# Two chained transformer blocks on one core: modulation sums moved ahead, first weights in places of their own

## The reference

```python
mod = c @ w_ada[l] + b_ada[l]                       # 1024 -> 6 * 1024, one vector
shift_m, scale_m, gate_m, shift_f, scale_f, gate_f = jnp.split(mod, 6, axis=-1)
h = modulate(rms_norm(x, g_pre_mix[l]), shift_m, scale_m)
proj = h @ w_in[l]                                  # q_a k_a v_a q_m k_m v_m o_m i_m f_m g_a g_m
...                                                 # rope, window attention; conv, silu, mLSTM
merged = sigmoid(g_a) * (y_a @ w_branch_attn[l]) + sigmoid(g_m) * (y_m @ w_branch_mlstm[l])
x = x + gate_m[:, None, :] * rms_norm(merged @ w_out[l], g_post_mix[l])
h2 = modulate(rms_norm(x, g_pre_ffn[l]), shift_f, scale_f)
ff = (silu(h2 @ w_ffn_gate[l]) * (h2 @ w_ffn_up[l])) @ w_ffn_down[l]
```

## Time and profile before

| | |
|---|---|
| median of 3 runs | 824.28 us (822.32 to 824.84) |
| the profiled execution | 825.46 us, of which the span of its trace is 823.7 us |
| PE busy | 773.9 us (94%) |
| DVE busy | 638.8 us (78%) |
| ACT busy | 393.4 us (48%) |
| moved from HBM | 171.60 MB, 210 GB/s over the span |

### The profile page before, as it was taken

How to read it: one execution, slowest core, us unless ns; L and a number is a source line. 1 busy time by engine, 2 the same in 40 slices (tenths; PEclk the granted TensorE clock), 3 DMA queues, 4 the chain that set the end, 5 groups by cost and what they waited for, 6 DMA issues and landing times.

```text
span 823.7 us, 15888 instructions
## 1 busy us (share of the span) xinstructions
PE 773.9 (94%) x6624; PEld 708.5 (86%) x6624; DVE 638.8 (78%) x840; ACT 393.4 (48%) x552; POOL 29.0 (4%) x44
## 2 busy tenths in 40 slices
PE   2879998999999999999999999989998999999996
PEld 2779988989878899999887988889878999999874
DVE  5857988988986987868886999886599777555456
ACT  3346755484455355443444795542225544444440
POOL 0200000000001000000001000040010000000000
PEclk9789999998999999999999999999999999999999
DMA  9794677583574999888992743600364679565621
GB/s 356 247 351 128 205 245 245 176 282 116 168 253 155 317 327 351 276 282 318 341 364 72 262 129 111 218 8 3 104 210 124 206 230 340 176 202 188 198 100 51
DMA packets 96021, 173.68 MB, mean 211 GB/s; under 512 B 7767, under 2 KB 55230, under 8 KB 95950
## 3 DMA queue, kind: packets, MB, share of 16 engines
q1 hardware_dynamic: 92848, 165.87, 60.7%
q0 software_dynamic: 1872, 5.86, 2.3%
q10 hardware_dynamic: 1230, 0.95, 0.3%
HBM read 171.60 MB, written 1.05 MB: 210 GB/s over the span
## 4 chain that ended last, share of the span: by engine, by line
PE 70%; DVE 18%; ACT 4%; DMA 3%; issue 3%; ACTq 1%; DVEq 0%; SPq 0%; POOL 0%; POOLq 0%
PE bank L2063 13%; PE bank L2064 12%; PE bank L2065 12%; PE bank L2328 4%; PE bank L2330 4%; PE bank L2329 4%; DVE wlo L448 3%; PE bank L2038 2%; PE bank L2039 2%; PE bank L2040 2%; DVE acc L475 2%; PE bank L2490 1%; DMA raw<-in_w_in 1%; DVE arena L475 1%; ACT whi L625 1%
## 5 line engine op out<-in xcount | busy, mean ns | idle before, releaser
L625 ACT ACTIVATE whi<-raw 128x1024 fp32r<-128x1024 f32 (+2 forms) x220 | 225.7, 1036 | 250.1 <-PE bank L2065 110.3
L448 DVE TENSOR_TENSOR wlo<-raw,whi 128x1024 fp32r<-128x1024 f32 (+2 forms) x220 | 259.7, 1195 | 94.3 <-ACT whi L625 90.6
L2063 PE MATMUL bank<-hh,whi 128*128 128x256 f32 x1016 | 287.0, 282 | 11.6 <-DVE wlo L448 8.6
L2064 PE MATMUL bank<-hl,whi 128*128 128x256 f32 x1016 | 284.2, 280 | 0.0
L2065 PE MATMUL bank<-hh,wlo 128*128 128x256 f32 x1016 | 284.1, 280 | 0.0
L2063 PEld LDWEIGHTS bank<-hh,whi 128*128 128x128 f32 x1016 | 192.8, 190 | 15.7 <-DVE wlo L448 7.8
L2064 PEld LDWEIGHTS bank<-hl,whi 128*128 128x128 f32 x1016 | 192.6, 190 | 0.5 <-issue 0.5
L2065 PEld LDWEIGHTS bank<-hh,wlo 128*128 128x128 f32 x1016 | 192.7, 190 | 0.0
L475 DVE SCALAR_TENSOR_TENSOR acc<-raw,cc,acc 128x1024 f32<-128x1024 f32 x56 | 71.7, 1281 | 6.1 <-DMA raw<-in_w_ada 3.7
L2328 PE MATMUL bank<-whi,ffh 128*128 128x512 f32 x168 | 65.7, 391 | 0.9 <-DVE wlo L448 0.9
L2330 PE MATMUL bank<-whi,ffl 128*128 128x512 f32 x168 | 65.5, 390 | 0.0
(11 more groups left out here) (445 smaller groups left out, 1051.7 us busy)
## 6 DMA issues: line engine op xcount, KB each, us to landing
raw<-in_w_ada SPq DMA_DIRECT2D x96, 512.0 KB, 5.2
raw<-in_w_in SPq DMA_DIRECT2D x54, 512.0 KB, 4.6
raw<-in_w_ffn_in SPq DMA_DIRECT2D x88, 256.0 KB, 3.9
raw<-in_w_ffn_gate SPq DMA_DIRECT2D x44, 256.0 KB, 4.5
raw<-in_w_ffn_up SPq DMA_DIRECT2D x44, 256.0 KB, 5.5
raw<-in_w_ffn_down SPq DMA_DIRECT2D x22, 512.0 KB, 5.3
raw<-in_w_ffn_out SPq DMA_DIRECT2D x22, 512.0 KB, 4.3
raw<-in_w_out SPq DMA_DIRECT2D x16, 512.0 KB, 4.4
```

The lines of the kernel that those rows point to most:

```text
L448: eng.tensor_tensor(lo[:, 0:nk * width], raw[:, b % RAW, 0:nk * width], hi[:, 0:nk * width].bitcast(fp), ALU.subtract)\
L625: act.activation(weight_place(g)[0][:, 0:nk * width], raw[:, b % RAW, 0:nk * width], ACT.Copy)\
L2063: mm(o, wh[:, k, c], xh[:, kk_, :], start=first, stop=False)
L2064: mm(o, wh[:, k, c], xl[:, kk_, :], start=False, stop=False)
```

## The change

It has five parts.

1. The 8 weight blocks of `o_if` get places of their own in a part of the arena that is free then (`FIRST = 8`), so their high halves wait for nothing, and the four shared places begin with `qm`.
2. `head` puts `c4` (part 2, first half) beside `qm`, `c5` beside `km`, `c6` and `c7` (part 3) beside `g2` and `g3`, `c8` beside `ba0`. Nothing stands beside `kva` and `g1`.
3. PE sums part 2 behind `g1` instead of behind `g2`, with 16 idle products around it, and part 3 behind `wo1` instead of ahead of `ba0`.
4. The constants and small vectors are issued by SP, two ahead of each of blocks 28 to 36, instead of by ACT; `x` is issued behind six blocks instead of two. ACT takes two small copies (`v1T`, `bmod`) from DVE.
5. The order ahead of `ba0` changes on PE, ACT and DVE, and there are fewer idle products at three places (`run_on` 22 to 16, 9 to 7, 18 to 13).

```diff
-    head = ["c0", "c1", "c2", "c3", "o_if", "qm", "km", "vm", "g0", "qa", "kva", "c8", "g1", "c4", "g2", "c5",
-            "g3", "c6", "ba0", "c7", "ba1", "bm0", "bm1", "wo0", "c9", "wo1"]
+    head = ["c0", "c1", "c2", "c3", "o_if", "qm", "c4", "km", "c5", "vm", "g0", "qa", "kva", "g1", "g2", "c6",
+            "g3", "c7", "ba0", "c8", "ba1", "bm0", "bm1", "wo0", "c9", "wo1"]
...
+        FIRST = 8
         def weight_place(g):
+            if g < FIRST:
+                at = [2112 + 576 * i for i in range(12)] + [15680 + 576 * i for i in range(4)]
+                return tuple(rounded(f"first{i}", at[i], [576]) for i in (2 * g, 2 * g + 1))
...
             for b, (_, _, nk, width, parts, _, _) in enumerate(order):
-                if b == 2:
+                if b == 6:
                     sp.dma_start(xt[:, :, :], A["x"][0].rearrange("(m p) n -> p m n", p=P)).then_inc(sem("x_in"), 16)
...
+                if 28 <= b < 37:
+                    for n in (2 * (b - 28), 2 * (b - 28) + 1):
+                        small_transfer(n)
...
-                    elif g >= HL:
+                    elif g >= HL + FIRST:
...
-            act.dma_start(cst[:, 258:CONST_N], A["const"][:, 258:CONST_N]).then_inc(sem("const_in"), 16)
-            act.dma_start(cc[:, 1, :], A["c_2"][0].rearrange("(p k) -> p k", k=8)).then_inc(sem("small_in"), 16)
-            vectors(1, ROWS2, v2)
...
-            scale_h(0, second_half)
-            prepare("o_if", slice(2, 4))
+            scale_h(0, second_half, lambda: prepare("o_if", slice(2, 4)))
...
+            part(2, lambda: run_on(4, 6))
+            run_on(4, 6)
             pe.wait_ge(sem("qr_ready"), 2)
...
-            pe.wait_ge(sem("piece_used"), 4)
-            intra_part(1, 4)
+            inter_part(1)
             turn_ya(1)
-            inter_part(1)
...
             rows_out("wo1", merged)
-            turn_h(1, lambda m: xn[:, m * D:(m + 1) * D], "xn_ready", 2, 18, 2 * (place["wo1"][0] % 2))
+            part(3)
+            turn_h(1, lambda m: xn[:, m * D:(m + 1) * D], "xn_ready", 2, 13, 2 * (place["wo1"][0] % 2))
```

More of the change, by code:

```diff
@@ L182, in build @@
         hreg = sb("hreg", [P, 4096])
+        made = {}
         def rounded(name, at, shape):
-            return nc.alloc_sbuf_tensor_at(name, [P] + shape, fr, offset=arena_at + 4 * at)
+            if name not in made:
+                made[name] = nc.alloc_sbuf_tensor_at(name, [P] + shape, fr, offset=arena_at + 4 * at)
+            return made[name]
         hh = rounded("hh", ARENA, [KT, S])
@@ L664, in _ @@
                    .then_inc(sem("xn_ready"), 1)
+            act.wait_ge(sem("vec_turned"), 2)
+            act.activation(v1T[:, :], bank[2][:, 0:n1], ACT.Copy).then_inc(sem("v1T_ready"), 1)
+            act.activation(bmod[:, 0, :], bank[2][:, P:P + 48], ACT.Copy).then_inc(sem("v1T_ready"), 1)
             split("o_if", slice(0, 4))
@@ L1263, in _ @@
             prepare("qa", slice(2, 4))
-            prepare("kva", slice(0, 5))
+            prepare("kva")
+            prepare("g1", slice(0, 1))
             def rotate_q(m):
@@ L1307, in _ @@
             dve.nop().then_inc(sem("arg_ready"), 1)
-            prepare("kva", slice(5, 6))
-            prepare("g1", slice(0, 1))
+            prepare("g1", slice(1, 2))
             dve.wait_ge(sem("cossin_ready"), 1)
@@ L1319, in _ @@
                 rotate_k(m)
+            collect_part(2)
             prepare("g2", slice(0, 3))
@@ L1441, in weigh_y, with split_ya @@
                    osig[:, m, :].rearrange("p (h n) -> p h n", h=HM), ALU.mult).then_inc(sem("ym_ready"), 1)
+            def split_ya(m):
+                t = slice(m * P, (m + 1) * P)
+                dve.wait_ge(sem("yah_ready"), m + 1)
+                TT(yal[:, :, t], bank[2 + m][:, :].rearrange("p (i n) -> p i n", i=4),
+                   yah[:, :, t].bitcast(fp), ALU.subtract).then_inc(sem("ya_split"), 1)
             take_inter(0)
-            collect_part(3)
-            prepare("ba1", slice(0, 1))
             divided(0)
@@ L1449, in _ @@
             divided(1)
+            split_ya(0)
+            prepare("ba1", slice(0, 1))
+            split_ya(1)
             head_shift(0)
+            take_inter(1)
             prepare("ba1", slice(1, 2))
-            gains(1, v1T[:, v1["g_pre_ffn"][0]:v1["g_pre_ffn"][1]])
-            for m in range(MT):
-                t = slice(m * P, (m + 1) * P)
-                dve.wait_ge(sem("yah_ready"), m + 1)
-                TT(yal[:, :, t], bank[2 + m][:, :].rearrange("p (i n) -> p i n", i=4),
-                   yah[:, :, t].bitcast(fp), ALU.subtract).then_inc(sem("ya_split"), 1)
-            take_inter(1)
             head_stats(1)
@@ L1543, in _ @@
                 dve.nop().then_inc(sem("x_added"), 1)
-                prepare("ff0", slice(m, m + 1))
+                if m:
+                    collect_part(3)
+                    gains(1, v1T[:, v1["g_pre_ffn"][0]:v1["g_pre_ffn"][1]])
+                else:
+                    prepare("ff0", slice(0, 1))
                 dve.wait_ge(sem("x_std"), m + 1)
@@ L2182, in _ @@
             pe.wait_ge(sem("s_masked"), 6)
-            part(2)
             for h2 in range(2):
@@ L2273, in _ @@
             inter_part(0)
-            part(3)
+            intra_part(1, 4)
             for h in range(HQ):
@@ L2311, in _ @@
             rows_out("wo1", merged)
-            turn_h(1, lambda m: xn[:, m * D:(m + 1) * D], "xn_ready", 2, 18, 2 * (place["wo1"][0] % 2))
+            pe.wait_ge(sem(f"pair{place['wo0'][0] % 2}_free"), place["wo0"][0] // 2 + 1)
+            part(3)
+            turn_h(1, lambda m: xn[:, m * D:(m + 1) * D], "xn_ready", 2, 13, 2 * (place["wo1"][0] % 2))
             def feed_forward(letter, down, n):
```

98 lines of the change are left out of this document (52 added, 46 removed).

## The result

The changed kernel takes 832.9 us (median of four runs, 831.4 to 835.4), the kernel before 823.6 beside it: a ratio of 1.0118, with a 95% interval of 1.0095 to 1.0141. I had forecast 823.5, with a range from 817.5 to 828.5. Later it was timed once more beside the experiments, at 831.5 us and a ratio of 1.0085 (1.0059 to 1.0111). So the change costs about 1%, some 8 us, and the likeliest case, the range and the sign of the sum were wrong. The profiled execution took 833.34 us, and the span of its trace is 831.5.

A forecast was written before the change was run, and what follows sets the result against it. PE, busy 94% of the span, was taken to set the end. Terms 0 + 1.0 + 1.4 + 0.7 - 1.7 - 2.2 + 0 made -0.8 us: 824.7 profiled, median 1.2 under the profiled time, so 823.5 us; range 817.5 to 828.5.

The forecast's parts named there:

- the likeliest case: Whole kernel: DVE becomes the bound and later gains about equal the clock's cost; 823.5 us, chance 0.40.
- DVE from qm to vm: From qm to vm: DVE takes eight more additions and becomes the bound, +1.0 us, between -3.7 and +2.9.
- The upper bound: From qm to vm: full DMA engines land c4's last block at about 57.5, so vm's low half ends at 82.2, +2.9 us.
- Start to o_if: Start to o_if: o_if may start up to 1.5 us earlier or later, costed at 0.
- The clock at vm: At vm: a wait of 3 us or more may slow PE's clock, 2.75 us or nothing; half taken, +1.4.
- kva and g1: At kva and g1: waits go, -2.9 us, and part 2 with 16 idle products comes in, +3.6; net +0.7.
- g2 to g3: From g2 to g3: part 2 leaves PE, the exponentials keep some of it; -1.7 us, could be -0.5.
- Ahead of ba0: Ahead of ba0: part 3 leaves and a product moves, 3.0 us, less 0.8 for a new wait; -2.2.
- Behind wo1: Behind wo1: part 3 comes in, 10 idle products and 0.52 us of idle time leave; +0.2, taken as 0.
- C: Rival ahead of vm: small loads on SP's queue make part 2's blocks late; +3.7 us, 828 us, chance 0.24.
- B: Rival ahead of vm: DVE is fed in time and its idle time takes the additions; 817.4 to 820.5 us, chance 0.36.

The follow-up runs named there:

- e1: Changed kernel with the 18 small loads issued by ACT again, between o_if and qm, and none by SP: 832.7 us, ratio 1.0072 to the kernel before.
- e10: Changed kernel with POOL's four broadcasts held back until the convolutions are done: 827.0 us, ratio 1.0032 to the kernel before.
- e14: e12 with part 2's blocks back beside qm (c4) and km (c5): 823.7 us, ratio 0.9996 to the kernel before.
- e12: Changed kernel, part 2's blocks beside kva and g1, ff0's old order, second gate's bias earlier, POOL's broadcasts held back, 16 fewer idle products: 819.4 us, ratio 0.9937.
- e7: Changed kernel with part 2's additions (c4, c5) done on only 8 of 1024 columns, values not right: 829.0 us, ratio 1.0064 to the kernel before.
- e8: Changed kernel with c4 and c5 loaded for only 16 of 128 partitions, values not right: 830.6 us, ratio 1.0069 to the kernel before.
- e6: Changed kernel with x loaded ahead of the third block again, not the seventh: 833.2 us, ratio 1.0103 to the kernel before.
- e5: Changed kernel with 34 idle products ahead of km and ahead of vm, in PE's waits: 834.1 us, ratio 1.0096 to the kernel before.
- e15: The changed kernel, unchanged, timed and profiled again: 831.5 us, ratio 1.0085 to the kernel before.
- e2: Changed kernel with ff0's second and third DVE blocks ahead of the scaling of h, as before: 828.7 us, ratio 1.0055 to the kernel before.
- e3: Changed kernel with part 2's blocks beside kva (c4) and g1 (c5), not qm and km: 823.5 us, ratio 0.9981 to the kernel before.

## Why the prediction was wrong

The sum was -0.8 us, and the two profiles have +7.8 and +8.5. Of these 8.6 and 9.3 us, 4.6 and 4.7 lie between o_if and vm and 6.2 and 3.0 behind ff0; the rest is small and partly cancels.

**The step that failed first: +1.0 us for DVE from qm to vm, chosen between -3.7 and +2.9.** Measured from o_if it is +5.6 and +5.7; vm's start itself came 3.5 and 6.9 us later. The upper bound was the better computation. I had c4's last block landing at 57.5 and its addition done at 58.8; the trace has that addition from 58.25 to 59.5, km's first low half at 64.28 (I had 63.6) and vm at 83.02 (upper bound 82.4). That the times fit so well is in part luck: o_if began 2.1 us earlier than before, and in the second profile, where it began 1.1 us later than before, vm came at 86.38. I had tied the landing of c4's last block to a fixed time of the trace, and it goes with o_if, whose blocks must leave the ring first: its addition ends 25.8 us behind o_if in one profile and 25.9 in the other. And I took a value below the bound, although I gave the full DMA engines as my reason to stay near it. DVE did start on qm's first block early, at 40.35 (43.85 in the second profile), and then idled for the next three. The earlier start was worth almost nothing, as e1 shows.

**What fills the window.** I counted the constants and POOL's loads as unchanged and left it there. They are 2.2 MB of the 9.3 MB that move between 34 and 62 us, and the 1.5 MB of the four broadcasts are read first behind 230 us. e10 shows that the broadcasts cost the changed kernel 4.4 to 4.6 us at vm. e14 against e12 shows what the place of part 2's blocks costs without them: 7.2 us for eight blocks more ahead of vm, through one ring in order, each with an addition of up to 1.28 us. How much of it are the bytes and how much the additions stays open: neither e7 nor e8 gives it back alone, and no run takes both away and leaves the blocks in their place.

**Start to o_if, taken as 0 "because DVE, not PE, sets vm below".** Wrong in its reason, and I had x's landing as what delays the turns of h, where it is the place of the rms rows (e6). DVE's work in o_if waits for PE's part 1, which waits for the idle products, so a late o_if is a late vm: vm lies 49.3 and 49.5 us behind it in both profiles, with o_if at 33.74 and at 36.93. The 32 idle products took 3.65 us in one and 5.90 in the other, and what decides between the two stays open.

**The clock at vm, +1.4, and kva and g1, +0.7.** Together 2.1; measured +2.2 and +2.7. e5 isolates the clock with 2.3 to 2.8 us, the upper of my two values: the waits ahead of km and vm were 4.26 and 4.22 us, and both were followed by 0.50. The Trainium skill, "TensorE: Matmul & The Clock Gate", section "HAM oscillation — how this bites in real kernels", has the product behind a wait for its operand start cold. At vm the trace agrees, and that was a better guide than my half. It is not so behind every wait: behind the 2.25 us inside ff1 in e15 the clock stayed at 1.00.

**g2 to g3, -1.7.** Measured -0.4 and -0.3. What part 2 frees is mostly taken by waits for ACT: that for the exponentials grew from 1.28 to 1.60 us, and a new one of 1.07 stands before it. I had named -0.5 as possible and priced the hope.

**Ahead of ba0, -2.2.** Right in kind: I had -3.0 and +0.8, measured are -3.1 up to ba0 and +1.6 up to wo0, of which 1.4 us is the new wait for y_m (L2324 in the waits above). **Behind wo1, 0**: wo0 to ff0 takes 27.24 us in both. Right.

**What I did not price at all: the order at ff0.** The diff has it, and my sum has no term for it, so it stood at nothing without a reason. The step to look for was who waits for the last low half of h: POOL, with two broadcasts and the bias, and behind them DVE and ff1. It cost 6.2 and 3.0 us, and in e2's trace that stage takes what it took before.

**The rivals.** C, slower at 828, had the right sign and the wrong cause (e1). I had given any time slower than the noise a chance of 0.24. B was wrong in this kernel; its vm at about 76 is what e3 reaches (75.85) by taking the blocks away from there.

## What to carry to other kernels

Before work is moved into a stretch in which an engine idles, look at what the idle engine waits for behind the first block: if the DMA engines are full there, removing the issuing engine's delay may only show the next one. List everything that is in flight in that stretch with the time of its first use, and move what is needed late before moving anything in. An edit of order that costs nothing where it stands has to be followed to every engine that waits for the delayed result, POOL's queue included.

## What the runs showed of the hardware

The same 32 idle products took 3.65 us in one execution and 5.90 us in another of the same kernel, with a granted clock of 1.00 recorded over both. From 26 to 28 us PE has 20 products in the one and 12 in the other, at the same recorded clock. So a recorded 1.00 was no proof of the pace in this place, and the count of products in a stretch was.

Blocks of 0.5 MB of w_in took 5.7 us from issue to landing (median of eight) with the stream and the constants in flight, and 7.5 us (median of seven) with POOL's four broadcasts beside them.

The clock fell to 0.50 behind waits of PE of 4.76, 4.26, 4.22 and 2.18 us in the first profile of the changed kernel, and did not behind waits of 2.25 and 1.84 us in the second.
